# Weights loaded at a step of two, tokens streamed backwards, and weight buffers at different places within 256 bytes

## The reference

```python
def swiglu(h, w_gate, w_up, w_down):          # first model; D_FF = 2816
    a = jnp.einsum('bsd,df->bsf', h, w_gate)
    u = jnp.einsum('bsd,df->bsf', h, w_up)
    return jnp.einsum('bsf,fd->bsd', jax.nn.silu(a) * u, w_down)

def _swiglu(x, w_in, w_out):                  # second model
    gate, up = jnp.split(x @ w_in, 2, axis=-1)
    return (jax.nn.silu(gate) * up) @ w_out
```

## Time and profile before

| | |
|---|---|
| median of 2 runs | 2814.77 us (2814.58 to 2814.96) |
| the profiled execution, first to last instruction | 2812.3 us |
| TensorE matmuls, weight loads | 15556 each, busy 2792.6 us (99%) and 2396.6 us (85%) |
| VectorE, ScalarE, GpSimd busy | 68%, 55%, 9% |
| HBM read | 500 MB, 178 GB/s over the span |

### The profile page before, as it was taken

One profiled execution on the slowest core, in us unless ns is written; L12 is line 12 of the kernel. 1 busy time (PEld: TensorE's weight loads), 2 busy tenths in 40 slices (PEclk: granted clock), 3 DMA queues, 4 the chain that ended last, 5 costly groups with the idle time before them and its releaser, 6 DMA issues.

```text
span 2812.3 us, 40293 instructions
## 1 busy us (share of the span) xinstructions
PE 2792.6 (99%) x15556; PEld 2396.6 (85%) x15556; DVE 1921.3 (68%) x3180; ACT 1554.0 (55%) x2718; POOL 241.5 (9%) x187
## 2 busy tenths in 40 slices
PE   9999999999999999999999999999999999999998
PEld 8889888888889888888888987888888888878887
DVE  6756676747655667756568777776566687777765
ACT  6545656545545656545456556455455465655553
POOL 0010011010010011010014100110100141001100
PEclk9999999999999999999999999999999999999999
DMA  6544445555544345555554344555555554445553
GB/s 242 191 171 158 149 156 182 193 185 190 195 167 152 139 172 194 199 190 195 195 193 179 136 163 159 210 194 182 199 189 195 183 187 153 158 156 184 209 185 135
DMA packets 75055, 503.82 MB, mean 179 GB/s; under 512 B 8784, under 2 KB 10480, under 8 KB 19184
## 3 DMA queue, kind: packets, MB, share of 16 engines
q1 hardware_dynamic: 74576, 501.07, 50.2%
q10 hardware_dynamic: 288, 0.17, 0.0%
HBM read 500.12 MB, written 1.08 MB: 178 GB/s over the span
## 4 chain that ended last, share of the span: by engine, by line
PE 93%; DVE 4%; POOL 2%; issue 1%; ACT 1%; DMA 0%; SPq 0%; DVEq 0%; ACTq 0%
PE ps L1544 45%; PE ps L1579 21%; PE ps L1585 11%; PE ps L1563 9%; PE ps L1606 3%; POOL wlo L2498 2%; DVE wlo L2038 1%; PE ps L1701 1%; PE ps L1699 1%; DVE conv L2327 1%; PE ps L1726 1%; PE ps L1716 0%; PE ps L1717 0%; PE ps L1718 0%; DVE ps L2144 0%
## 5 line engine op out<-in xcount | busy, mean ns | idle before, releaser
L1777 ACT ACTIVATE whi<-raw 128x1024 fp32r<-128x1024 f32 (+3 forms) x938 | 977.5, 1045 | 600.3 <-PE ps L1544 426.1
L2038 DVE TENSOR_TENSOR wlo<-raw,whi 128x1024 fp32r<-128x1024 f32 (+2 forms) x894 | 1084.1, 1220 | 219.9 <-ACT whi L1777 218.9
L1579 PE MATMUL ps<-xT_both,whi 128*128 128x512 f32 x2560 | 641.6, 393 | 0.0
L1544 PE MATMUL ps<-whi,xT_both 128*128 128x512 f32 (+2 forms) x2336 | 628.9, 391 | 2.6 <-DVE xT_both L2061 1.6
L1579 PEld LDWEIGHTS ps<-xT_both,whi 128*128 128x128 f32 x2560 | 461.1, 189 | 82.6
L1544 PEld LDWEIGHTS ps<-whi,xT_both 128*128 128x128 f32 x2336 | 425.5, 188 | 83.7 <-issue 9.3
L1585 PEld LDWEIGHTS ps<-xT_both,wlo 128*128 128x128 f32 x2560 | 349.3, 191 | 24.9
L1585 PE MATMUL ps<-xT_both,wlo 128*128 128x256 f32 x2560 | 357.1, 282 | 0.0
L1544 PE MATMUL ps<-wlo,xT_both 128*128 128x512 f32 (+2 forms) x1168 | 354.6, 385 | 0.3 <-DVE wlo L2038 0.3
L2118 DVE TENSOR_TENSOR h<-h,ps 128x256 f32<-128x256 f32 x320 | 127.0, 418 | 203.1 <-ACT h L1826 203.1
L1544 PEld LDWEIGHTS ps<-wlo,xT_both 128*128 128x128 f32 x1168 | 218.4, 188 | 43.7 <-DVE wlo L2038 1.4
(11 more groups left out here) (315 smaller groups left out, 2526.7 us busy)
## 6 DMA issues: line engine op xcount, KB each, us to landing
raw<-in_w SPq DMA_DIRECT2D x435, 1024.0 KB, 4.8
vr<-in_vrows SPq DMA_DIRECT2D x19, 512.0 KB, 5.6
raw<-in_w SPq DMA_DIRECT2D x12, 768.0 KB, 4.3
raw<-in_w SPq DMA_DIRECT2D x10, 896.0 KB, 4.5
sums<-scratch SPq DMA_DIRECT2D x8, 512.0 KB, 4.4
raw<-in_w SPq DMA_DIRECT2D x4, 832.0 KB, 4.4
raw<-in_w SPq DMA_DIRECT2D x4, 576.0 KB, 3.7
raw<-in_w SPq DMA_DIRECT2D x4, 512.0 KB, 6.9
```

Of the source, the lines that this page charges most:

```text
L1544: made = e.matmul(bank[:, 0:c1 - c0], xs[:, kt, sl], ws[:, j * w + c0:j * w + c1], start=kt == 0 and n == 0, stop=kt == job.nk - 1 and n == 2)
L1579: e.matmul(bank[:, :].rearrange("p (n x) -> p n x", n=2), hi[:, o:o + 128], job.xt.both[:, :, kt, :], start=kt == 0, stop=False, skip_grou ...
L1777: e.activation(out, raw, ACT.Copy).then_inc(*mark("hi", i))
L2038: e.tensor_tensor(out, raw, hi.bitcast(F32), sub).then_inc(*mark("lo", i))
```

## The change

Three edits. The packing on the host puts the gate and the up columns of FFN chunks 1 to 20 alternately (gate 0, up 0, gate 1, up 1, ...), and `wide` takes the stationary operand with a step of two elements. In `wide`, `columns` and `dt_rows` the tokens are streamed from the last to the first (`::-1`), and the output is written backwards with them, so that each result stands where it stood. And nine fillers of 32 bytes stand ahead of the weight buffers: `whi0` to `whi4` begin 0, 32, 64, 96 and 128 bytes, `wlo0` to `wlo4` 160, 192, 224, 256 and 288 bytes past the places they had within 256 bytes. The activations keep the place of `whi0`. `rows` is not edited.

```diff
+def woven(key):
+    return key[1] == "up" and key[3] > 0
@@
-    many("whi", NHL, [128, PIECE], F32R)
     at_line = nc.sbuf_base % LINE
-    many("wlo", NHL, [128, PIECE], F32R)
+    for name, fills in (("whi", (0, 8, 8, 8, 8)), ("wlo", (8, 8, 8, 8, 8))):
+        m[name] = []
+        for i, n in enumerate(fills):
+            if n:
+                sbuf(f"{name}{i}_fill", [128, n])
+            m[name].append(sbuf(f"{name}{i}", [128, PIECE], F32R))
@@ columns
-                    made = e.matmul(out, ws[:, o:o + 128], xs[:, kt, :], start=kt == 0 and n == 0 and c % 2 == 0,
+                    made = e.matmul(out[:, ::-1], ws[:, o:o + 128], xs[:, kt, ::-1], start=kt == 0 and n == 0 and c % 2 == 0,
@@ wide
-                o = j * w + 128 * c
-                e.matmul(bank[:, :].rearrange("p (n x) -> p n x", n=2), hi[:, o:o + 128], job.xt.both[:, :, kt, :],
+                o = j * w + c
+                e.matmul(bank[:, :].rearrange("p (n x) -> p n x", n=2)[:, :, ::-1], hi[:, o:o + 255:2],
+                         job.xt.both[:, :, kt, ::-1],
@@
-                o = j * w + 128 * c
-                made = e.matmul(bank[:, 256:512], lo[:, o:o + 128], job.H[:, kt, :], start=False,
+                o = j * w + c
+                made = e.matmul(bank[:, 256:512][:, ::-1], lo[:, o:o + 255:2], job.H[:, kt, ::-1], start=False,
@@ dt_rows
-                made = e.matmul(job.outs[0][0:16, 0:256], ws[:, kt * w:kt * w + w], xs[:, kt, :],
+                made = e.matmul(job.outs[0][0:16, 0:256][:, ::-1], ws[:, kt * w:kt * w + w], xs[:, kt, ::-1],
@@ kernel, packing of the weights on the host
+            if woven(key):
+                pairs = dst[:, first:off].reshape(128, len(kts), 2, 128)
+                dst[:, first:off] = pairs.transpose(0, 1, 3, 2).reshape(128, -1)
```

## The result

The changed kernel takes 2845.5 us (median of 2 runs), the kernel before 2814.77: a ratio of 1.0109, 95% interval 1.008 to 1.0138. It is about 31 us slower, which is clear of noise and under 2%. The profiled executions differ by 31.6 us (2843.9 against 2812.3).

The account below looks back on a forecast made before the run. The prediction took PE's matmul pace as the bound. Its terms, 0 + 0 + 9.3 + 0 = +9.3 us on 2814.8, gave 2824 us, with the sum's own range 2805 to 2845 and a forecast range of 2725 to 2915 us.

Parts of the forecast that it names:

- What bounds the kernel: Whole kernel: PE is busy 99% of the span, so only matmul pace or a new wait can move the time.
- Step (1): The 5120 loads of `wide` at a step of two: taken as 0 us, bounds nothing or 258 us.
- Step (2): Backward streams and outputs on 7328 matmuls: taken as 0 us, bounds nothing or one more cycle for each column.
- The output at half rate: Backward outputs in `wide` and `columns` cost one more cycle a column: 1055 us, 3870 us in all; chance 0.06.
- Step (3): Buffers at different places, including about 6000 matmuls of `rows`: 0.7 ns on each of 6000 + 7328, 9.3 us.
- Step (4): ACT and DVE writing weight halves to places 32 bytes apart: PE would still not wait, 0 us.
- The signs: Paces to look for in the chain afterwards, such as `rows` at 226 to 231 ns, each tied to a cause.
- The quarrel ends: The faster rival: stream and load stop hindering each other in `wide` and `columns`, 88 us less, 2727 us; chance 0.15.
- The quarrel grows: Slower rival: the 13.3 ns excess doubles for all 7328 edited matmuls, 97 us more, 2912 us; `rows` unchanged; chance 0.13.
- The two half-rate rivals: In `wide`, loads at half rate, 3073 us, chance 0.10; there and in `columns`, outputs at half rate, 3870 us, 0.06.
- A fixed price of the change of weights: All matmuls: the roughly 13 ns over the columns' time is paid per stationary operand change, which no layout can remove.

Follow-up runs that it names:

- the map: Computation left out against the kernel before; TensorE runs only matmuls at varied places, widths and directions; 48 of 512 columns at distance 0 took 10.88 us.
- second map: Another kernel without the computation, matmuls only, with more widths and stretches in the order of `wide`; 48 of 512 columns at distance 0 took 10.90 us.

## Why the prediction was right or wrong, point by point

- **What bounds the kernel**: right. No engine and no wait came into it; all of the 31 us is in the pace of the matmuls.
- **Step (1), load with a step of two, 0 us**: no load took twice its time; lo went from 119.1 to 119.5 ns with this edit alone. But I looked for the cost in the load's own time only. It came in the stream beside it: hi 230.0 to 233.9 ns, 10 us, +10.9 for the edit alone. That term was mis-sized by its whole.
- **Step (2), backwards, 0 us**: +4.0 alone, made of +8 in hi, −2 in lo, −3 in `columns`. The output at half rate didn't come; the output's direction is free.
- **Step (3), places, +9.3 us**: that the places cost time was right and the sign too, the size wrong, 23.5. My reason was half right: I took the 416-column row because its places alternate, but one place that never changes costs as much (+28.9 us). I took 0.7 ns a matmul from the 416- and 288-column rows and it was 5.3 in the down projections. Those rows were poor witnesses: by the starts, matmuls of 416 columns went from 188.0 to 189.7 ns in the changed kernel and those of 288 from 133.2 to 132.9, and in the map the price at 320 and 384 is zero (7.03 and 7.04 us, 8.32 and 8.32 us for 48 at distances 0 and 32 bytes). A price that depends on the width can't be read from another width. The upper bound I gave, 30 us from the 3.7 ns of `wide` hi, was the better row: same width, other state.
- **Step (4), ACT and DVE, 0 us**: right. DVE's total is 1923 us against 1921, ACT's 1554.5 against 1554.0.
- **The sum**, 2824 us with its own range of 2805 to 2845: the median is 0.5 us past that range's end and well within 2725 to 2915. The sum named a third of the 31 us. What carried the forecast is the argument that no half rate comes, so that only a few ns a matmul are in play; the wide range did the rest. That 2% is about what a measurement can tell was too cautious: the runs of one kernel lie within 1.4 us of each other.
- **The signs**: "if `rows`, which isn't edited, slows, it is the buffers' places" pointed to the right edit, with 232.1 ns against the 226 to 231 that I had allowed.
- **The quarrel ends, 0.15**: not by this change. Yet its sign "for it", the two paces of hi, was real and worth 8 us, in an edit that nobody could see in the rows: one direction for 512 columns and the other for 256.
- **The quarrel grows, 0.13**: this is the side on which the time moved, by 31 us instead of 97. As a quarrel that doubles in `wide` and `columns` it didn't come: `columns` got faster, and at 512 columns a shorter load doesn't shrink the excess. But the part that the change moved is a matter between stream and load: a step of two in the load alone slows the stream beside it, and the price of the place goes when the load reads one element. Its main place was `rows`, which this rival held to be safe.
- **The two half-rate rivals**: neither came. A half rate exists, but for a stream at a step of two (453 ns), which this change doesn't have.
- **"A fixed price of the change of weights"**, the argument against the faster rival: wrong in the main. The 13.3 ns at 256, 288 and 512 columns, found again at 320 and 384, are no proof of it: at the same place it is 20 at 448, with a shorter load it is anything from 6.7 to 18.4, and with a stream that reads nothing new 5.4 are left, with bf16 2.5. Only those can be a fixed price.

## What to carry to other kernels

When TensorE is the bound and its operands have four bytes, the distance of the stream's start from the stationary operand's start within 256 bytes is a tuning knob: here it is worth 3% of every matmul of 512 columns, and nothing at 384 in the map (1 ns in the kernel, 174.2 to 175.3). Keep operands that stream 512 columns at distance zero and forwards, and try backwards for those of 256. Weights loaded at a step of two cost little by themselves (lo: 0.4 ns) but slow a 512-column stream beside them (hi: 3.9 ns); streams at a step cost double. To price such an edit, look for a row of the same width in another state rather than one of another width, and measure the pace of a stream in a kernel that has nothing else.

## What the runs showed of the hardware that I had not expected

- A stream's pace depends on what ran ahead of it, over some five matmuls (second map, behind 256-column ones): 233, 236, 228, 233, 231, then 226 to 227 ns.
- A matmul of 512 bf16 columns takes 215.8 ns; of 4-byte ones 226.7 to 238, by place alone (238 at a distance of 4 bytes).
- The clock fell although PE counted as busy throughout. In the second map, 48 matmuls of 64 columns, each with a load of 128, ran at 112 ns; 4.8 us into this stretch the granted clock fell to its lower level, 1.2 GHz, and came back 37.5 us later, after stretches of 64 and 128 columns and within one of 192. It is one execution. The windows of that kernel, with the busy time of PE, PEld, ACT and POOL, then PE's clock, the DMAs' share and GB/s:

```profile
30.00:57.00 27.00, 27.00 (x150) 26.77 (x148) 0.00 (x0) 0.00 (x0) 0.62 0.01 1
57.00:67.00 10.00, 10.00 (x48) 10.00 (x48) 0.00 (x0) 0.00 (x0) 0.50 0.00 0
81.00:87.00 6.00, 6.00 (x53) 6.00 (x52) 0.00 (x0) 0.00 (x0) 1.00 0.00 0
```

At the lower level the matmuls of 64 and of 128 columns both took 213.3 ns each, nearly twice the 112 of the 64-column ones ahead, so what set their pace is not their columns but what both have, a load of 128. The kernels of this case show nothing of it: both have the full clock in all 40 slices.
